# Expert weights in four sets of buffers that go round, in place of three and one used once: a two-layer trunk with mixture of experts

## What is computed

```
def moe_ffn(h, router_w, router_bias, w_gate, w_up, w_down):
    ...
    y = jnp.zeros_like(h)
    for e in range(N_EXPERTS):
        a = jax.nn.silu(h @ w_gate[e]) * (h @ w_up[e])
        y = y + gates[:, e:e + 1] * (a @ w_down[e])
    return y

def reference(...):
    for i in range(DEPTH):
        ...
        x = x + g1 * yl
        hl = modulate(rms_norm(x, norm2_g[i]), sh2, sc2).reshape(b * n, d)
        ...
        x = x + g2 * y.reshape(b, n, d)
    return rms_norm(x, final_norm_g)
```

## Time and profile before

| | us |
|---|---|
| median of three runs | 1149.12 |
| lowest, highest | 1147.08, 1150.25 |
| the profiled execution | 1146.06 |
| its span in the trace | 1144.2 |

### The profile page before, as it was taken

The page is one execution under the profiler, slowest core; times in us unless marked ns, Lnnn a source line. Parts: engine busy times, 40 slices in busy tenths (PEclk is TensorE's granted clock), DMA queues, the critical chain, the costliest instruction groups (busy, mean ns, idle before and its releaser), DMA issues.

```text
span 1144.2 us, 25209 instructions
## 1 busy us (share of the span) xinstructions
PE 1004.0 (88%) x10134; PEld 660.9 (58%) x10135; DVE 411.6 (36%) x881; ACT 336.5 (29%) x755; POOL 173.1 (15%) x257
## 2 busy tenths in 40 slices
PE   4799999988889988799899649999999866999875
PEld 2577777544555565467566447888454643555543
DVE  1533331355843542122122273212862721323212
ACT  3532221366741211011111255323861110111111
POOL 0000000000000024244344300920000010112100
PEclk9999999999999999899899869999999897999988
DMA  9866664998240579999999467222627889699994
GB/s 338 303 219 221 221 210 171 346 355 314 109 199 18 208 280 399 422 421 424 422 424 415 172 248 164 94 74 104 264 60 306 335 320 425 253 381 425 424 423 188
DMA packets 90811, 317.58 MB, mean 278 GB/s; under 512 B 20094, under 2 KB 32135, under 8 KB 78451
## 3 DMA queue, kind: packets, MB, share of 16 engines
q1 hardware_dynamic: 84594, 303.04, 69.0%
q0 software_dynamic: 5280, 10.36, 2.4%
q10 hardware_dynamic: 864, 3.15, 0.7%
HBM read 311.05 MB, written 9.54 MB: 280 GB/s over the span
## 4 chain that ended last, share of the span: by engine, by line
PE 73%; DMA 14%; DVE 4%; issue 4%; ACT 3%; SPq 1%; DVEq 0%; ACTq 0%; POOLq 0%
PE ps L2031 25%; PE ps L1772 21%; PE ps L1927 7%; DMA expert_sets<-in_moe_w_up_dram 7%; PE ps L1669 5%; PE ps L1693 3%; DMA expert_sets<-in_moe_w_down_dram 2%; DMA ring<-in_ada_w_dram 2%; PE ps L2053 2%; PE ps L1827 1%; PE ps L1854 1%; DMA ada_late<-in_ada_w_dram 1%; PE ps L1883 1%; PE ps L1710 1%; DMA moe<-h_rows,slot_idx 1%
## 5 line engine op out<-in xcount | busy, mean ns | idle before, releaser
L2031 PE MATMUL ps<-expert_sets,moe 128*32 128x256 f32 x6304 | 363.7, 390 | 54.1 <-issue 31.2
L2031 PEld LDWEIGHTS ps<-expert_sets,moe 128*32 128x32 f32 x6304 | 226.5, 113 | 186.7 <-issue 76.5
L1772 PE MATMUL ps<-w_high,x_high 128*128 128x512 f32 x352 | 141.4, 402 | 6.6 <-DVE x_low L508 5.1
L1618 DVE STREAM_TRANSPOSE moe<-moe 128x256 f32<-128x256 f32 x68 | 44.7, 657 | 263.8 <-PE ps L2031 257.2
L1772 PE MATMUL ps<-w_high,x_low 128*128 128x512 f32 x352 | 137.9, 392 | 0.0
L1772 PE MATMUL ps<-w_low,x_high 128*128 128x512 f32 x352 | 137.7, 391 | 0.0
L1125 ACT ACTIVATE moe<-ps 128x128 f32<-128x128 f32 x68 | 18.9, 277 | 327.5 <-PE ps L2031 325.9
L495 DVE TENSOR_TENSOR w_low<-ring,w_high 128x2048 fp32r<-128x2048 f32 x24 | 56.2, 2350 | 132.5 <-ACT w_high L492 132.5
L1772 PEld LDWEIGHTS ps<-w_high,x_high 128*128 128x128 f32 x352 | 66.5, 189 | 30.5 <-issue 14.8
L779 POOL MEMSET moe<- 128x128 f32 x2 | 0.4, 204 | 534.9 <-PE ps L1953 534.9
L797 POOL DMA_INDIRECT moe<-h_rows,gather_idx x66 | 68.4, 1037 | 52.2 <-POOL gather_idx L843 27.7
(11 more groups left out here) (261 smaller groups left out, 1143.1 us busy)
## 6 DMA issues: line engine op xcount, KB each, us to landing
expert_sets<-in_moe_w_down_dram SPq DMA_DIRECT2D x32, 2048.0 KB, 18.4
expert_sets<-in_moe_w_gate_dram SPq DMA_DIRECT2D x30, 2048.0 KB, 15.9
expert_sets<-in_moe_w_up_dram SPq DMA_DIRECT2D x30, 2048.0 KB, 21.0
ring<-in_ada_w_dram SPq DMA_DIRECT2D x16, 2048.0 KB, 8.0
ring<-in_diff_w_qkv_dram SPq DMA_DIRECT2D x6, 2048.0 KB, 9.3
ada_late<-in_ada_w_dram SPq DMA_DIRECT2D x6, 2048.0 KB, 12.4
ring<-in_na_w_qkv_dram SPq DMA_DIRECT2D x6, 2048.0 KB, 8.9
rows<-mod_rows SPq DMA_DIRECT2D x11, 512.0 KB, 7.3
```

The lines of the kernel that those rows point to most:

```text
L1618: dve.transpose(blk_inT, blk_in[b].rearrange("p (j k) -> p k j", k=KC)).then_inc(m_xt[l], 1)
L1772: mm = pe.matmul(ps[:, n % 2], x_part[:, k, tok], w_part, start=(k == 0 and i == 0), stop=(k == KC - 1 and i == 2))
L2031: mm = pe.matmul(ps[g * SLOTS:(g + 1) * SLOTS, bank, 0:n_out], lhs_T[:, k, :], weights(k, g), start=(k == 0), stop=(k == n_chunks - 1), sk ...
```

## The change

Every place takes the set p % 4, and the fourth set is whole: gate and up stay in `extra`, and a new buffer `extra_down` lies over 15 KB of new room, `mod_rows` and the first 128 columns of the constants, where `cos` and `sin` now stand. The room comes from the area for DMA descriptors, which shrinks to 1,024 bytes a partition. p = 3's down is loaded ahead of the plan, in layer 0 behind the second store of `mod_rows`, in layer 1 behind the output strips. SP's loads from p = 4 on are one loop, each waiting for p - 4. TensorE's loop has four places (4 to 7) and three passes in both layers; the written-out places 13 to 15, `last_expert` and its `keep_busy(8)` are gone. The first strip of layer 1 waits for the gates of p = 14 in place of its downs, and the strips' slots move by one. Two details of the diff move nothing in time order: `keep_busy` reads other columns of the constants, and the scattered rows stand ahead of strips 1 and 2 as they did.

```
-        expert_sets = over("expert_sets", 0, [P, 3, 3, KC * STRIP])
...
+        extra_down = over("extra_down", ARENA_KB + 16, [P, FF // P, D])
...
+        sb("extra_down_room", [P, KC * STRIP - 2 * P])
+        mod_rows = sb("mod_rows", [96, P])
...
-                    add_qkv(g, (i + 2) % 3)
+                    add_qkv(g, i % 3)
...
+        def loads(l, p, rounds=0):
+
+            return 16 * (p // SETS + 1 + rounds + l * (N_EXP // SETS))
...
-            def later_parts(l, p, which, ws, back=3):
+            def later_parts(l, p, which):
 
                 e = expert_at(l, p)
-                for w in ws:
+                blocks = sp.value_load(plan[0:1, bass.ds(p + 1 - SETS, 1)], min_val=1, max_val=MAX_BLOCKS)
+                for w in range(3):
                     if w != 1:
-                        blocks = sp.value_load(plan[0:1, bass.ds(p + 1 - (3 if w == 2 else back), 1)], min_val=1, max_val=MAX_BLOCKS)
                         sp.wait_ge((m_gu, m_gu, m_dn)[w][l], blocks + (w == 2))
                         sp.sem_inc(s_turn_sp, 1)
-                    expert_weights(l, w, e, which[w == 2])
+                    expert_weights(l, w, e, which)
...
-                later_parts(l, EXTRA + 1, (gate_set(EXTRA + 1), None), (0, 1), back=4)
-                later_parts(l, EXTRA, (None, EXTRA % 3), (2,))
-                later_parts(l, EXTRA + 1, (None, (EXTRA + 1) % 3), (2,))
-                for p in range(5, 7):
-                    later_parts(l, p, (gate_set(p), p % 3), (0, 1, 2), back=4)
-                with sp.Fori(0, (N_EXP - 7) // 3) as i:
-                    for p in range(7, 10):
-                        later_parts(l, 3 * i + p, (gate_set(p), p % 3), (0, 1, 2))
+                with sp.Fori(0, N_EXP // SETS - 1) as i:
+                    for s in range(SETS):
+                        later_parts(l, SETS * i + SETS + s, s)
...
-            last_blocks, n0 = load_experts(0)
-            sp.wait_ge(m_dn[0], last_blocks + 1)
+            sp.wait_ge(s_modD, 32)
+            expert_weights(0, 2, EXTRA, EXTRA)
+            blocks, pairs = load_experts(0)
+            sp.wait_ge(m_gu[0], blocks)
             load_strip(1, 0)
-            load_expert_rows(0, n0)
-            blocks = sp.value_load(plan[0:1, N_EXP:N_EXP + 1], min_val=N_EXP, max_val=MAX_BLOCKS)
-            sp.wait_ge(m_gu[0], blocks)
+            load_expert_rows(0, pairs)
...
+            expert_weights(1, 2, EXTRA, EXTRA)
             sp.wait_ge(s_qm[1], len(qkv_jobs[1]))
...
-                def last_expert(p, first, end):
-
-                    down_loaded(p - 1)
-                    downs(first - 1, (p - 1) % 3)
-                    sum_rows(first)
-                    keep_busy(8)
-                    gates_loaded(p)
-                    gates_ups(first, gate_set(p))
...
-                with pe.Fori(0, (N_EXP - 4) // 3 - l) as three:
...
-                    expert(6, end_2, end_3, three)
-                if l == 1:
-                    end_0, end_1 = block_end(N_EXP - 4), block_end(N_EXP - 3)
...
-                    last_expert(N_EXP - 1, end_2, end_3)
+                with pe.Fori(0, N_EXP // SETS - 1) as i:
...
+                    expert(SETS + 3, end_3, end_4, i)
...
-    nc = bacc.Bacc("TRN2", target_bir_lowering=False, num_devices=1)
+    nc = bacc.Bacc("TRN2", target_bir_lowering=False, num_devices=1, dynamic_dma_scratch_size=1024)
```

More of the change, by code:

```diff
@@ L72 @@
 H_KB, R_KB, EXTRA_KB, ARENA_KB = 144, 160, 168, 184
-EXTRA = 3
+SETS, EXTRA = 4, 3
 TILES_OF = [list(range(TILES)), list(range(CTX_TILES, TILES))]
-CONST_PARTS = [("ident", P), ("mirror", P), ("before", P), ("slot", SLOTS), ("half", 1), ("block", BLK_COLS), ("sort", N_EXP), ("rev_expert", N_EXP),
-               ("rev_group", N_GRP), ("token", TILES), ("dest", 2 * TILES), ("cos", 2 * 32), ("sin", 2 * 32),
+CONST_PARTS = [("cos", 2 * 32), ("sin", 2 * 32), ("ident", P), ("mirror", P), ("before", P), ("slot", SLOTS), ("half", 1), ("block", BLK_COLS), ("sort", N_EXP), ("rev_expert", N_EXP),
+               ("rev_group", N_GRP), ("token", TILES), ("dest", 2 * TILES),
                ("valid", GRID_W), ("invalid", GRID_W)]
@@ L184, in build_trunk @@
         mod = sb("mod", [P, LAYERS, 48, 2])
-        mod_rows = sb("mod_rows", [96, P])
         rw = sb("rw", [P, KC, N_EXP])
@@ L362, in build_trunk @@
         s_idx = [sem(f"plan_ready_{l}") for l in range(LAYERS)]
-        m_wl = [[sem(f"expert_{w}_loaded_{s}") for w in ("gate", "up", "down")] for s in range(3)]
-        s_extra = sem("extra_parts_loaded")
+        m_wl = [[sem(f"expert_{w}_loaded_{s}") for w in ("gate", "up", "down")] for s in range(SETS)]
         s_keep = sem("residual_rows_kept")
@@ L456, in expert_part @@
         def expert_part(w, which):
+            if which == EXTRA:
+                return extra_down[:] if w == 2 else extra[:, w].rearrange("p (k n) -> p k n", n=STRIP)
             return expert_sets[:, which, w, :].rearrange("p (k n) -> p k n", n=D if w == 2 else STRIP)
         def gate_and_up(which, k, g):
-            return (extra[:] if which == "extra" else expert_sets[:, which, 0:2])[:, :, k * STRIP + g * FG:k * STRIP + (g + 1) * FG]
+            return (extra[:] if which == EXTRA else expert_sets[:, which, 0:2])[:, :, k * STRIP + g * FG:k * STRIP + (g + 1) * FG]
         def wait_strip(eng, l, j):
@@ L587, in build_trunk @@
         N_KEPT = [4, 1]
-        def gate_set(p):
-            return p if p < EXTRA else "extra" if p == EXTRA else (p - 1) % 3
-        def nth_load(w, p):
-            used = [q for q in range(N_EXP) if (q % 3 if w == 2 else gate_set(q)) == (p % 3 if w == 2 else gate_set(p))]
-            return used.index(p) + 1, len(used)
+        def loads(l, p, rounds=0):
+            return 16 * (p // SETS + 1 + rounds + l * (N_EXP // SETS))
         VECTOR_LOADS = 7
@@ L1709, in keep_busy @@
                 for _ in range(count):
-                    pe.matmul(ps[:, 3, 0:2 * P], ident, cst[:, 0:2 * P], start=True, stop=True)
+                    pe.matmul(ps[:, 3, 0:2 * P], ident, cst[:, P:3 * P], start=True, stop=True)
             for a in range(ADA_QKV):
@@ L2066, in gates_loaded @@
                 def gates_loaded(p, rounds=0):
[L2068 removed]
                     for w in range(2):
[L2070 removed]
+                        pe.wait_ge(m_wl[p % SETS][w], loads(l, p, rounds))
                 def down_loaded(p, rounds=0):
[L2074 to L2075 removed]
+                    pe.wait_ge(m_wl[p % SETS][2], loads(l, p, rounds))
                 def block_end(p):
                     return pe.value_load(plan[0:1, bass.ds(p + 1, 1)], min_val=1, max_val=MAX_BLOCKS)
[L2081 to L2103 removed]
+                def expert(p, first, end, rounds=0, then=None):
+                    gates_loaded(p, rounds)
+                    gates_ups(first, p % SETS)
                     after = None if then is None else block_end(then)
                     down_loaded(p - 1, rounds)
[L2106 removed]
+                    downs(first - 1, (p - 1) % SETS)
                     sum_rows(first)
@@ L2111, in expert @@
                         with pe.Fori(first + 1, end) as i:
-                            gates_ups(i, gate_set(p))
-                            downs(i - 1, p % 3)
+                            gates_ups(i, p % SETS)
+                            downs(i - 1, p % SETS)
                             sum_rows(i)
@@ L2157, in _ @@
                 if l == 0:
-                    downs(n - 1, 0)
+                    downs(n - 1, (N_EXP - 1) % SETS)
                     unread(m_gu[0])
```

33 lines of the change are left out of this document (6 added, 27 removed).

## The result

The changed kernel takes 1164.2 us (median of four runs, 1163.9 to 1167.2) where the kernel before took 1148.1 beside it (four runs, 1142.1 to 1150.3): ratio 1.0155, 95% interval 1.0112 to 1.0197. It is slower, by 1.6%. The profiled execution took 1164.02 us, its span is 1162.2.

What follows compares the result with a forecast made beforehand. Both expert stages were taken as a race between TensorE and the weights. Loads -6.5 and -14.3, refetched code +35, sum +14.2 us; 1146.06 + 14.2 + 3.06 = 1163.3 us, 8 in 10 range 1126 to 1173.

Steps and rivals of the forecast that it cites:

- Place 3's down weights early: Both layers: loading them early costs nothing on the path; without the cover, one load, 5.1 to 5.5 us.
- step 2: Layer 0's loads: one load fewer behind the plan and a 0.7 us queue hole gone, -6.5 us.
- Layer 0, -6.5: Layer 0's expert stage: loads from place 5 on land 6.2 us sooner, place 10's wait goes; bounds -4 and -7.5.
- Layer 1's loads, -14.3: Layer 1's expert stage: place 9's gate, not place 8's, waits for place 5's six blocks; the end comes 14.3 us sooner.
- Place 7's first jump: Layer 1: place 7, first time in the loop behind a one-block place, pays 5.0 us, the mean of earlier first jumps.
- The eight products and the last place: Layer 1's place 15: dropping keep_busy(8) and the reordered last expert costs nothing, or 2.6 us behind a wait.
- Strips and room: Layer 1's output strips with changed slots, and a sixteenth of the descriptor room: no change.
- Code fetched again in layer 1, not in layer 0: TensorE's longer loop overflows its code store; seven jumps in passes two and three at 5.0 us, +35; bounds 0 and 43.
- rival of stalls that shrink: Within the partly refetched case, 0.15: code stalls shrink to 3 us because the weights' queue is emptier; 1148 us.
- Works as said: Rival, 0.31: all code is kept and only the load terms count, -20.8 us, 1128.3 us.
- Partly refetched: Rival, 0.15: only the loop's ends collide, or stalls shrink to 3 us; -0.8 us in all, 1148 us.
- descriptor room: Rival, 0.03: with too little room GpSimd's gathers and scatters wait for earlier ones to land, costing over 100 us.

Runs made afterwards that it cites:

- late_down: The changed kernel with TensorE's place code written once, and place 3's down weights loaded at their old point in both layers: 1128.0 us, ratio 0.9800 to the kernel before.
- rewritten pair: TensorE's code of a place written once instead of twice, in the kernel before (three sets): 1134.3 us, and in the changed kernel (four sets): 1121.4 us.
- merge_loop1: The changed kernel with TensorE's place code written once in layer 1's loop alone: 1133.2 us, ratio 0.9870 to the kernel before.
- small_before: The kernel before with descriptor room of 1024 and layer 1's last place done as the others, without the eight products: 1153.2 us, ratio 1.0016.
- pad_before: The kernel before with 192 never-run instructions behind each of three places of TensorE's layer 1 loop, spanning 7.9 pieces: 1183.1 us, ratio 1.0278.
- pad_40: The kernel before with 160 never-run instructions behind each of three places of TensorE's layer 1 loop, spanning 7.4 pieces: 1194.6 us, ratio 1.0384.
- merge_after: The changed kernel (four sets) with TensorE's code of a place written once: 1121.4 us, ratio 0.9782 to the kernel before.

## Why the prediction was right

It forecast 1163 (1163.3 by its sum) and 1164.2 was measured, by the mechanism that it named: more loads ahead, and a loop whose code is fetched again in layer 1 alone. It had given that case 0.43. Two stretches that it put at nothing grew by 1.7 and 3.0 us and the two that it worked out differ from it by +1.4 and -3.1, so that the total is as near as it is partly by luck. Point by point:

1. *Place 3's down weights early: nothing.* On the path of the time ahead of the stage that holds. Inside the stages it may be worth something: layer 1's is 3.1 us longer without it (late_down), though the whole times don't show it. For layer 0 the prediction had this under the loads of step 2 ("one load fewer behind the plan"); for layer 1 it had it nowhere.
2. *Layer 0, -6.5.* The stage got 5.1 us shorter (5.6 in the rewritten pair), and place 15's gates began 4.7 us sooner where 6.3 was said. Sign, place and mechanism were right; the load came at 625.9, not 624.0. The bounds were -4 to -7.5.
3. *Layer 1's loads, -14.3.* In the changed kernel the term is seen only as a difference: the tail grew by 17.6, and without the 32.4 us of point 6 it would be 14.8 shorter. merge_loop1 has the tail at 117.0 in place of 130.4, so -13.4, but with other code in the loop and without the dear first jump that the -14.3 had in it. The rewritten pair, with the places' code written alike, shows 8.7. So the size holds for this kernel and not for a compact one; why it is smaller there no run took apart. Place 8 and place 9 wait as said. Place 7's first jump was taken at 5.0 us; in the changed kernel the sums around it stand 11.40 apart, 5.0 over the pitch, of which 3.25 are waiting and 1.7 the clock (5.35 us for 64 products in place of 3.66):

```profile
1010.31 1.15 PE L2044 MATMUL ps<-moe 32*128 32x256 f32 x16
1014.71 5.35 PE L2022 MATMUL ps<-extra,moe 128*32 128x256 f32 x64 [3.25 <-issue]
...
1021.71 0.50 PE L2044 MATMUL ps<-moe 32*128 32x256 f32 x4
```

4. *The eight products and the last place: nothing, unless a wait is left.* Right: in the changed kernel no wait is left, and where one is the products took 2.1 us more (small_before), with 2.6 forecast.
5. *Strips and room: nothing.* The room shows no price (small_before). The strips were not tried by themselves; the stretch between the stages rose by 1.7 us, within its scatter.
6. *Code fetched again in layer 1, not in layer 0: +35.* Right in kind and nearly in size, wrong in how it is made up. By the sums' distances, with 1.8 us of a loop head taken off each way back, the two ways back cost 8.5 and 10.1 us, places 8, 10, 12 and 14 0.3, 4.3, 6.1 and 0.8, the way out 1.6, and a straight stretch of place 9 0.7: 32.4 in place of 7 x 5.0. That the sum holds is luck in part: only two of the seven jumps cost near the mean of 5.0, two cost under 1 us and two over 8. The cheap ones fall where the DMA engines stand nearly idle, which is what the prediction's rival of stalls that shrink had in mind; a mean over first-pass jumps beside full traffic could not show it. merge_loop1 gives 26 for the same, 31.0 less place 7's 5.0; it has some stalls of its own (2.34 us at a way back), and a TensorE that is late finds its weights there.

The head grew by 3.0 us where nothing was said. The rewritten pair, with little code to wait for, differs by 1.1 there, so most of it is probably code that falls otherwise in its pieces; no run took that apart.

*The rivals.* "Works as said" at 1128 is near what merge_loop1 shows at 1133.2, with the code out of the way in that loop alone. "Partly refetched" falls here with the twenty pieces of the last two passes, ten in 1034:1096 and ten in 1096:1150, as many as two whole passes take; pad_before shows that such a case exists. The descriptor room falls with small_before. Of the signs that were named, over 70 pieces, their place in the second and third pass, place 8's gate near 960 and no wait at place 10 came as said. Place 15's gates in layer 0 began 4.7 us sooner and not 6, the waits behind places 7 and 11 were over 7 us, and those behind places 8 and 14 did not reach 3.

The limit of the store, which the prediction said was in no row, is now measured from both sides: between 6.7 and 7.4 pieces for a loop. The Trainium skill (Runtime: NRT & Kernel Launch, Instruction fetch mechanics) calls TensorE's instruction memory a FIFO of 128 KB, 2048 instructions, refilled in blocks of 16 KB. The runs agree on the size, if one of the eight pieces is the one fetched ahead. They agree with a FIFO too in pad_40, where the loop is fetched anew in each pass, but not plainly in pad_before, whose third pass fetched nothing for 27 us.

## What to carry to other kernels

Count TensorE's instructions in a loop (an f32 matmul of the program is two matmuls and two weight loads in the trace) before a loop is made longer. A loop of 6.7 pieces of some 250 was kept here; those of 7.4 and more were fetched again in at least one pass, and then a jump backwards waited 6 to 15 us and some jumps forwards 3 to 8, clock not counted. Place code that differs in a small part behind a branch rather than writing the whole twice: here the branch cost nothing that shows and the second copy did, also in the kernel of three sets, whose loop fits.

Room for code is a resource that the profile shows only by its traffic, and a change that pays for room in SBUF with it looks free. The lines to look at are the instruction queue's count, and waits put down to "issue".

## What the runs showed of the hardware

- TensorE keeps a loop of 6.7 pieces of 16 KB and fetches one of 7.4 again in every pass: 57 against 75 pieces, 1151.6 against 1194.6 us, for 64 instructions more a place. A loop of 7.9 pieces was fetched again in its second pass and hardly in its third (69 pieces).
- A jump backwards to code that is not there waits 7.2 and 7.7 us in the changed kernel, 13.3 and 7.9 in pad_before, 15.0 and 9.5 in pad_40; jumps forwards wait from nothing to 8.4. A wait at the head of a loop whose code is there takes 2.4 us (merge_after, no piece on q8 from 1012 to 1110), and a jump inside a block shows nothing.
- Behind such a wait the next products run at half clock (0.50 from 1042.80 to 1045.60), 1.6 to 1.7 us more each time.
- Code written twice costs 12 us in the first places of layer 1, in the kernel of three sets (92.4 to 80.8) as in that of four (93.6 to 81.9), most likely by jumps over 0.9 of a piece that has not come yet.
- The hint at the loop's head changed neither the number of pieces (72) nor the time (1.0138 against 1.0155, intervals that overlap).
